# Packing 64 routed experts into 32 blocks of rows instead of 40, gathering four blocks at once, and spreading a normalisation over softmax groups

## The chip, the core and the metric

The kernel runs on one core of a Trainium2 chip. TensorE (PE) multiplies, VectorE (DVE), ScalarE (ACT) and GpSimd (POOL) do the rest, SyncE (SP) issues most DMAs; each runs its own instruction stream and they meet at semaphores. The metric is the device time of one execution in microseconds; the median of three before was 2076.38 us (2073.79 to 2079.16).

## The reference, cut to what matters

Two layers run over 384 tokens (128 context, 256 latent), width 1024, all in float32.

```
h = x * (1 + sc1) + sh1;  q,k,v,gate... = h @ w_in            # 1024 x 2816
ya = retention(4 heads x 64), both directions
     o = (o - mean) / sqrt(var + eps) per head; ya = (o * gn_g + gn_b) * silu(gate)
yb = windowed attention (6 heads),  yc = neighbourhood attention (6 heads)
x  = LN(alpha * x + g1 * (concat(ya, yb, yc) @ w_out))
h  = x * (1 + sc2) + sh2
scores = sigmoid(h @ w_router); 6 of 64 experts a token, group limited
routed = sum over the chosen e of  w_e * (silu(h @ gate_e) * (h @ up_e)) @ down_e
x  = LN(alpha * x + g2 * (routed + shared expert))
```

An expert has a 1024 x 512 matrix for gate and up (2 MB) and a 256 x 1024 matrix for down (1 MB). There are 384 x 6 = 2304 assignments a layer, 36 an expert on average.

## The kernel before, in words

A hardware loop runs the layer twice. A layer has these stages: modulation vectors, the combined input projection, retention, twelve softmax groups (each three heads of one 128-token tile; the first four groups are the context tile with 128 keys, the other eight have 384), the output projection, the first norm, routing, the routed experts with the shared one among them, and the second norm. Nothing is planned at run time: each engine's order is written out by hand, and waits are placed by semaphore.

**Retention's norm.** DVE evicts the state (L1209), and then runs the per-head norm of all three tiles in one go: mean (L1215), subtract, square, sum (L1219), variance (L1220), a square root on ACT (L1632), reciprocal and four multiplies and adds (L1222 to L1229). Only then does it start on the softmax groups, whose row maxima it takes with `peak` (L1238) and whose outputs it scales with `weigh` (L1257). ACT computes silu of the gate (L1630) and the root just ahead of its softmax work. PE has already computed the scores of groups 0 and 1 (L835) and waits with the transposes of group 0's weights (L856) for ACT's exponentials.

**Routing.** Experts 0 to 3 get a block of 128 rows each, at once (`PRE = 4`). The others are ordered by their count of tokens, highest first. DVE writes for each assignment a place; POOL scatters 36 / 2 = 18 columns of entries to a table in DRAM with one indirect DMA each (L1768), reads the table back (L1777), and DVE turns it into row indices (`take_slots`, L1439, L1440). An expert that gets more rows than its room sends the rest to further table columns, and if any has, a second loop over 3 x 64 blocks runs.

**The experts.** `BLOCKS` lists 40 blocks of 128 rows. After the four first ones, a pattern of 1, 2, 2 experts a block repeats: an expert alone has 128 rows of room, one of a pair has 64. For block b PE runs, in this order: `gate_up(b)` (L975: eight steps of k, one matmul for each expert of the block, its rows as weights, the expert's matrix as 512 moving columns, output to the partitions of its rows), `turn_rows(b+1)` (L961: transposes of the gathered rows), `down_rows(b-1)` (L1000), `turn_hidden(b)` (L985), and in twelve of the blocks a step of the shared expert (L1013 to L1025). ACT applies silu (L1703) and evicts the transposed rows (L1695, L1696), DVE multiplies (L1466), evicts the hidden rows (L1475) and the outputs (L1482, L1483). POOL gathers the rows of block b+2 (L1752) after the transposes of block b, and scatters the outputs of block b-1 (L1758). The four first gathers stand in POOL's stream as 0, 1, then eight of the 18 table scatters, 2, eight more, 3, and the last two.

**Weights.** SP loads gate and up into a ring of four 2 MB buffers (`NG`, L610) and down into six 1 MB buffers (`ND`, L614), in one stream: for block b it waits for `gate_up(b)`, issues the ring loads that go into the buffers which this frees, then waits for `down_rows(b-1)` and issues the down loads that this frees. Load n of the ring thus waits for `gate_up` of the block that holds load n-4. At block 36 SP also loads 2 MB of vectors for the second norm (L598, L600), at block 6 the shared expert's 3 MB. A matmul in float32 is two instructions in the trace.

## Time and profile before

| | |
|---|---|
| median of three runs | 2076.38 us |
| the profiled execution, time | 2074.37 us |
| the profiled execution, span | 2072.3 us |
| mean granted TensorE clock | 0.892 |
| PE busy | 82% of the span |
| HBM read, written | 573.53 MB, 48.81 MB |

The span runs from the first to the last instruction; the profiled execution's own time is 2.1 us more. The two layers take about half of the span each; in the page's 40 slices (51.8 us each) the experts of the first layer lie in slices 8 to 18 and those of the second in 28 to 38. Busy time of PE counts pipelined matmuls and is no measure of how near the array is to its peak.

### The profile page before, as it was taken

The numbers are of one execution on the slowest core, as the hardware profiler recorded it, in microseconds if no ns is written. First come the engines' busy times: TensorE is split into PE (matmuls) and PEld (weight loads), VectorE is DVE, ScalarE is ACT, GpSimd is POOL, SyncE is SP. The second block draws the span as 40 slices with busy tenths as digits, with TensorE's granted clock in tenths as the row PEclk, the third lists the DMA queues.
The fourth block names the chain that finished last, engine by engine and source line by source line (L and its number), as shares of the span: only waits on it lengthen the run. The fifth ranks groups of instructions, "written<-read, shape, count | busy, mean of one in ns | idle before, by whom it ended". The sixth has DMA issues, their size and how long they took to land. (4 is left out here: it accounts for less than half of the span.)

```text
span 2072.3 us, 19838 instructions
## 1 busy us (share of the span) xinstructions
PE 1692.1 (82%) x7193; PEld 875.9 (42%) x7193; DVE 593.9 (29%) x1190; ACT 340.2 (16%) x668; POOL 227.5 (11%) x228
## 2 busy tenths in 40 slices
PE   3897888779798999997348969887897989999953
PEld 1685563534333343342117746545433333433421
DVE  1525324621111111111615353255211111111116
ACT  0322341101110111010012224411110100101100
POOL 0000000141111111110000000002311111111100
PEclk8898699689899999999659987987898999999986
DMA  7634318179999999995475343171799999999944
GB/s 294 188 119 145 135 37 307 57 262 369 422 410 416 402 393 424 405 402 208 183 272 158 127 175 124 51 320 67 255 401 422 413 396 410 401 422 386 415 168 175
DMA packets 119282, 576.95 MB, mean 278 GB/s; under 512 B 46252, under 2 KB 48828, under 8 KB 78088
## 3 DMA queue, kind: packets, MB, share of 16 engines
q1 hardware_dynamic: 93992, 534.38, 64.9%
q0 software_dynamic: 25120, 41.13, 5.4%
q8 instruction: 62, 1.02, 0.2%
q14 instruction: 44, 0.36, 0.1%
q10 hardware_dynamic: 64, 0.07, 0.0%
HBM read 573.53 MB, written 48.81 MB: 300 GB/s over the span
## 5 line engine op out<-in xcount | busy, mean ns | idle before, releaser
L975 PE MATMUL bank<-ring,arena_a 128*64 128x512 f32 (+1 forms) x2048 | 592.3, 621 | 92.6 <-DMA ring<-in_w_expert_gu 89.0
L975 PEld LDWEIGHTS bank<-ring,arena_a 128*64 128x64 f32 (+1 forms) x2048 | 216.7, 156 | 424.1 <-issue 424.1
L1000 PE MATMUL bank<-arena_b,arena_a 128*64 128x512 f32 (+1 forms) x704 | 237.3, 604 | 2.7 <-DVE arena_a L1475 2.7
L1466 DVE SCALAR_TENSOR_TENSOR arena_a<-arena_a,slot_w,bank 128x256 f32<-128x256 f32 x80 | 38.5, 481 | 589.7 <-ACT arena_a L1703 583.0
L1758 POOL DMA_INDIRECT scratch_y<-arena_a,slot_idx x80 | 80.4, 1005 | 889.8 <-DVE arena_a L1483 889.2
L1703 ACT ACTIVATE arena_a<-bank 128x256 f32<-128x256 f32 x80 | 30.7, 384 | 889.8 <-PE bank L975 889.8
L1482 DVE COPY arena_a<-bank 128x512 f32<-128x512 f32 x80 | 55.3, 692 | 316.6 <-PE bank L1000 316.6
L760 PE MATMUL bank<-win_hi,xmT_hi 128*128 128x512 f32 (+1 forms) x288 | 110.0, 382 | 27.3 <-DVE arena_a L1122 24.6
L1000 PEld LDWEIGHTS bank<-arena_b,arena_a 128*64 128x64 f32 (+1 forms) x704 | 78.7, 154 | 101.4 <-issue 98.2
L1000 PE MATMUL bank<-arena_a 128*64 128x512 f32 (+1 forms) x320 | 116.4, 597 | 0.0
L761 PE MATMUL bank<-win_hi,xmT_lo 128*128 128x512 f32 (+1 forms) x288 | 110.5, 384 | 0.0
L961 PE MATMUL bank<-cst,arena_a 128*128 128x128 f32 x640 | 89.5, 285 | 25.4 <-DMA arena_a<-scratch_x,slot_idx 25.4
L762 PE MATMUL bank<-w_lo,xmT_hi 128*128 128x512 f32 (+1 forms) x288 | 110.0, 382 | 0.0
L961 PEld LDWEIGHTS bank<-cst,arena_a 128*128 128x128 f32 x640 | 73.6, 145 | 81.1 <-issue 54.3
L1752 POOL DMA_INDIRECT arena_a<-scratch_x,slot_idx x80 | 83.9, 1048 | 103.6 <-DVE slot_w L1383 54.8
L897 PE MATMUL bank<-ring,xmT 128*128 128x512 f32 x192 | 86.3, 613 | 7.5 <-ACTq L1670 7.5
L706 PE MATMUL bank<-ring,condT 128*2 128x512 f32 x384 | 61.3, 751 | 29.8 <-DMA ring<-in_w_mod 29.8
L1113 DVE TENSOR_TENSOR w_lo<-ring,win_hi 128x2048 fp32r<-128x2048 f32 (+1 forms) x24 | 55.6, 2318 | 80.0 <-ACT win_hi L1584 80.0
L760 PEld LDWEIGHTS bank<-win_hi,xmT_hi 128*128 128x128 f32 x288 | 55.3, 192 | 40.1 <-issue 24.8
L1695 ACT ACTIVATE arena_a<-bank 128x512 f32<-128x512 f32 x80 | 47.8, 597 | 122.1 <-PE bank L961 122.1
L1077 PE MATMUL bank<-ring,cst 128*128 128x512 f32 x72 | 36.4, 662 | 35.8 <-DMA ring<-scratch_y 31.7
L1584 ACT ACTIVATE win_hi<-ring 128x2048 fp32r<-128x2048 f32 (+1 forms) x24 | 42.3, 1771 | 134.9 <-PE bank L762 70.6
(263 smaller groups left out, 1710.2 us busy)
## 6 DMA issues: line engine op xcount, KB each, us to landing
ring<-in_w_expert_gu SPq DMA_DIRECT2D x128, 2048.0 KB, 18.7
arena_b<-in_w_expert_down SPq DMA_DIRECT2D x88, 1024.0 KB, 21.3
ring<-in_w_mod SPq DMA_DIRECT2D x24, 2048.0 KB, 7.7
arena_a<-in_w_expert_down SPq DMA_DIRECT2D x40, 1024.0 KB, 19.8
ring<-in_w_in SPq DMA_DIRECT2D x10, 2048.0 KB, 13.2
ring<-in_w_out SPq DMA_DIRECT2D x4, 2048.0 KB, 8.3
ring<-scratch_y SPq DMA_DIRECT2D x4, 2048.0 KB, 10.8
ring<-scratch_y SPq DMA_DIRECT2D x8, 1024.0 KB, 17.1
```

Source lines behind the costliest of these rows:

```text
L706: ins = pe.matmul(bank[32 * j:32 * j + 2, :], condT[:, k, :], w[:, k % 2, CH * j:CH * j + CH], start=(k == 0), stop=False)
L760: pe.matmul(out, hi[:, k, :], win_hi[:, k, cols], start=(k == 0), stop=False)
L761: pe.matmul(out, lo[:, k, :], win_hi[:, k, cols], start=False, stop=False)
L762: ins = pe.matmul(out, hi[:, k, :], w_lo[s][:, k, cols], start=False, stop=(k == KD - 1))
L897: ins = pe.matmul(bank[:, :], xmT[:, k, P * t:P * t + P], w[:, k, :], start=(k == 0), stop=(k == KD - 1))
L961: ins = pe.transpose(psum[2 + k // 4][:, P * (k % 4):P * (k % 4) + P], xg[b % 2][:, P * k:P * k + P], ident)
L975: ins = pe.matmul(psum[b % 2][w * i:w * i + w, :], xT[:, k, w * i:w * i + w], ring_view(gu_slot(n))[:, k, :], start=(k == 0), stop=(k == K ...
L1000: ins = pe.matmul(psum[5 + f][w * i:w * i + w, :], hT[b % 2][:, k, w * i:w * i + w], down[n % ND][:, k, CH * f:CH * f + CH], start=(k == 0 ...
L1113: dve.tensor_tensor(w_lo[s][:, ks, cols], ring_view(s)[:, ks, cols], win_hi[:, ks, cols].bitcast(F32), ALU.subtract).then_inc(win_lo_ready, 1)
L1482: dve.tensor_copy(ys[b % 2][:, 0:CH], psum[5][:, :])
L1752: pool.indirect_dma_start(xg[b % 2], None, scratch_x, bass.IndirectOffsetOnAxis(ap=slot_idx[:, 0, b:b + 1], axis=0), bounds_check=TOK - 1, ...
L1758: pool.indirect_dma_start(scratch_y, bass.IndirectOffsetOnAxis(ap=slot_idx[:, 1, b:b + 1], axis=0), ys[b % 2], None, bounds_check=TOK * TO ...
```

## The change

The first part is the plan of blocks: 32 blocks, of kind 1 (one expert, 128 rows), kind 2 (two of 64) and kind 3 (one of 64 and two of 32), after the four first ones. Ranks 4 to 11 get 128 rows, 12 to 39 get 64, 40 to 63 get 32. In a kind 3 block all matmuls are 32 rows wide, four for each step of k; the expert with 64 rows takes two of them. The rings stay as they are.

```diff
-    for _ in range(6):
-        for size in (1, 2, 2, 1, 2, 2):
...
+    blocks = [[(n, P)] for n in range(PRE)]
+    wide, half, third = iter(range(PRE, 12)), iter(range(12, 40)), iter(range(40, E))
+    for _ in range(4):
+        for kind in (3, 1, 3, 2, 3, 1, 2):
+            if kind == 1:
+                blocks.append([(next(wide), P)])
+            elif kind == 2:
+                blocks.append([(next(half), 64), (next(half), 64)])
             else:
-                blocks.append([paired, paired + 1])
-                paired += 2
+                blocks.append([(next(half), 64), (next(third), 32), (next(third), 32)])
...
-SHARED_AT = {13 + 2 * n: (n // 4, n % 4) for n in range(4 * TILES)}
-SHARED_LOAD, NORM_LOAD = 6, 36
+SHARED_AT = {8 + 2 * n: (n // 4, n % 4) for n in range(4 * TILES)}
+SHARED_LOAD, NORM_LOAD = 5, 29
...
+            def block_tiles(b):
+                loads, sizes = block_loads(b), [rows for r, rows in BLOCKS[b]]
+                w = min(sizes)
+                of_tile = [n for n, rows in zip(loads, sizes) for _ in range(rows // w)]
+                return [(n, w * i, w) for i, n in enumerate(of_tile)]
...
                     for k in range(KD):
-                        for i, n in enumerate(loads):
-                            ins = pe.matmul(psum[b % 2][w * i:w * i + w, :], xT[:, k, w * i:w * i + w], ring_view(gu_slot(n))[:, k, :],
+                        for n, r, w in block_tiles(b):
+                            ins = pe.matmul(psum[b % 2][r:r + w, :], xT[:, k, r:r + w], ring_view(gu_slot(n))[:, k, :],
                                             start=(k == 0), stop=(k == KD - 1))
```

`down_rows` changes in the same way. The second part: the four first gathers are issued at once, ahead of the table's scatters, into four buffers (the two of before and two that held the first norm's gates).

```diff
+            def gather_of(b):
+                if b < PRE:
+                    return (xg + [gateb[:, 0, :], gateb[:, 1, :]])[b], first_gathered[b], 16
+                return xg[b % 2], gathered[b % 2], 16 * ((b - PRE) // 2 + 1)
...
-                gather(0)
-                gather(1)
+                for b in range(PRE):
+                    gather(b)
...
-                    if j in (7, 15):
-                        b = 2 + j // 8
-                        pool.wait_ge(xT_full, b - 1)
-                        gather(b)
```

The third: for the last block `down_rows` of the block before comes ahead of `gate_up` on PE, and `rows_out` ahead of `hidden` on DVE.

```diff
+                    if b == NB - 1:
+                        down_rows(b - 1)
                     gate_up(b)
                     if b + 1 < NB:
                         turn_rows(b + 1)
-                    if b:
+                    if 0 < b < NB - 1:
```

The fourth: retention's norm becomes nine steps, one behind each softmax group's `weigh`; ACT takes silu of the gate ahead of retention, and the root behind the exponentials of group 5.

```diff
                     if g:
                         weigh(g - 1)
+                        retention_norm(g - 1)
...
+                    if g == 5:
+                        act.wait_ge(var_ready, 1)
+                        act.activation(var, var, ACT.Sqrt).then_inc(root_ready, 1)
```

Steps 0 to 3 are mean, subtract, square, variance; 4 is empty; 5 is reciprocal and multiply; 6 and 7 the learned scale and shift; 8 the multiply by the gate.

## Rows read from the trace of the kernel before

**Rows 1.** The page: DMA issues; count, KB each, median us to landing.
```profile
ring<-in_w_mod SPq DMA_DIRECT2D x24, 2048.0 KB, 7.7
```
**Rows 2.** Windows; columns PE, PEld, DVE, ACT, POOL busy, PE clock, DMA share, GB/s.
```profile
413.70:500.00 86.30, 73.16 (x247) 33.01 (x248) 18.86 (x31) 9.68 (x20) 29.70 (x29) 0.92 0.78 289
500.00:940.00 440.00, 405.32 (x1620) 166.01 (x1618) 71.40 (x136) 46.70 (x96) 62.65 (x62) 0.97 0.99 410
```
**Rows 3.** Waits of PE, 403 to 985: us in total, times, longest.
```profile
PE bank L975 <- DMA ring<-in_w_expert_gu: 43.8, 11, 11.0
```
**Rows 4.** Timeline of PE: a block of one expert, and the next, a pair.
```profile
464.90 7.03 PE L975 MATMUL bank<-ring,arena_a 128*128 128x512 f32 x16
...
476.39 7.09 PE L975 MATMUL bank<-ring,arena_a 128*64 128x512 f32 x32
```
**Rows 5.** Timeline of PE around the gathers of blocks 2 and 3.
```profile
414.66 7.11 PE L975 MATMUL bank<-ring,arena_a 128*128 128x512 f32 x16 [0.60 <-issue]
432.06 1.97 PE L961 MATMUL bank<-cst,arena_a 128*128 128x128 f32 x8 [10.29 <-DMA arena_a<-scratch_x,slot_idx]
433.82 5.76 PE L1000 MATMUL bank<-arena_b,arena_a 128*128 128x512 f32 x8
```
**Rows 6.** Timeline of POOL: first scatter of the table, and its reading back.
```profile
410.58 1.02 POOL L1768 DMA_INDIRECT slots<-arena_a,place_i  x1 [10.52 <-DVE place_i L1429]
...
438.72 0.60 POOL L1777 DMA_DIRECT2D arena_a<-slots  x1 [1.42 <-DMA slots<-arena_a,place_i]
```
**Rows 7.** Groups by line and form: weight loads of 64 and of 2 columns.
```profile
L975 PEld LDWEIGHTS bank<-ring,arena_a 128*64 128x64 f32 x1536 | 119.9, 144 | 305.7 <-issue 305.7
L706 PEld LDWEIGHTS bank<-ring,condT 128*2 128x2 f32 x384 | 7.4, 88 | 56.7 <-DMA ring<-in_w_mod 39.4 <-issue 15.4
```
**Rows 8.** Timeline of PE: 16 matmuls over four groups of 32 columns.
```profile
198.05 1.90 PE L706 MATMUL bank<-ring,condT 128*2 128x512 f32 x16
```
**Rows 9.** Timeline of PE: gate_up after waits for weights, and the layer's end.
```profile
534.57 10.05 PE L975 MATMUL bank<-ring,arena_a 128*64 128x512 f32 x32 [11.03 <-DMA ring<-in_w_expert_gu]
...
963.59 8.88 PE L975 MATMUL bank<-ring,arena_a 128*64 128x512 f32 x32 [7.20 <-DMA ring<-in_w_expert_gu]
...
977.61 3.65 PE L1000 MATMUL bank<-arena_b,arena_a 128*64 128x512 f32 x16 [1.34 <-DVE arena_a L1475]
```
**Rows 10.** Timeline of SP at the end of the experts.
```profile
929.95 0.91 SPq L598 DMA_DIRECT2D arena_b<-mods  x2
...
936.95 1.32 SPq L610 DMA_DIRECT2D ring<-in_w_expert_gu  x1
```
**Rows 11.** Timeline of all engines between retention and softmax.
```profile
202.03 0.68 DVE L1209 TENSOR_SCALAR arena_b<-bank 64x512 f32<-64x512 f32 x1 [3.51 <-PE bank L815]
...
211.69 0.68 DVE L1238 TENSOR_REDUCE cmisc<-bank 128x1 f32<-128x128 f32 x3
214.18 0.90 PE L856 MATMUL bank<-cst,arena_b 128*128 128x128 f32 x3 [11.31 <-ACTq L1661]
```
**Rows 12.** Windows of the softmax stage, columns as in rows 2.
```profile
226.00:247.00 21.00, 20.92 (x85) 13.75 (x85) 5.38 (x17) 4.29 (x16) 0.00 (x0) 0.50 0.29 101
```
**Rows 13.** Timeline of DVE: peak, and a group's weigh at either clock.
```profile
226.38 0.36 DVE L1257 TENSOR_TENSOR arena_a<-bank,cmisc 128x192 f32<-128x192 f32 x1 [3.74 <-PE bank L870]
236.97 0.36 DVE L1257 TENSOR_TENSOR arena_a<-bank,cmisc 128x192 f32<-128x192 f32 x1 [3.07 <-PE bank L870]
...
257.77 0.36 DVE L1257 TENSOR_TENSOR arena_a<-bank,cmisc 128x192 f32<-128x192 f32 x1 [3.40 <-PE bank L870]
259.37 0.56 DVE L1238 TENSOR_REDUCE cmisc<-bank 128x1 f32<-128x384 f32 x1 [1.24 <-PE bank L847]
...
266.33 0.36 DVE L1257 TENSOR_TENSOR arena_a<-bank,cmisc 128x192 f32<-128x192 f32 x1 [3.60 <-PE bank L870]
```
**Rows 14.** Timeline of ACT, second layer: waits for DVE's decay, silu's table.
```profile
1208.91 0.62 ACT L1620 ACTIVATE arena_b<-cst,cmisc 128x384 f32<-128x384 f32 x1 [5.05 <-DVE arena_b L1193]
...
1220.81 1.28 ACT L1630 ACT_TABLE_LOAD   x1
```

More of the change, by code:

```diff
@@ L40, in plan_blocks @@
 def plan_blocks():
-    blocks = [[n] for n in range(PRE)]
-    alone, paired = PRE, PRE + 12
-    for _ in range(6):
-        for size in (1, 2, 2, 1, 2, 2):
-            if size == 1:
-                blocks.append([alone])
-                alone += 1
-            else:
-                blocks.append([paired, paired + 1])
-                paired += 2
-    assert alone == PRE + 12 and paired == E
+    blocks = [[(n, P)] for n in range(PRE)]
[6 more added lines that the diff above has]
+                blocks.append([(next(half), 64), (next(half), 64)])
+            else:
+                blocks.append([(next(half), 64), (next(third), 32), (next(third), 32)])
+    assert all(next(left, None) is None for left in (wide, half, third))
     return blocks
@@ L59 @@
 NB = len(BLOCKS)
-LOADS = [r for b in BLOCKS for r in b]
+LOADS = [r for b in BLOCKS for r, rows in b]
 BLOCK_OF = [n for n, b in enumerate(BLOCKS) for r in b]
@@ L138, in constants @@
     for n, b in enumerate(BLOCKS):
-        for i, r in enumerate(b):
-            cap[r], row[r], col[r] = P // len(b), P // len(b) * i, n
+        for i, (r, rows) in enumerate(b):
+            cap[r], row[r], col[r] = rows, sum(other for _, other in b[:i]), n
     put("cap", cap[:, None])
@@ L426, in build @@
             gathered, scattered = [sem("gathered0"), sem("gathered1")], [sem("scattered0"), sem("scattered1")]
+            first_gathered = [sem(f"first_gathered{b}") for b in range(PRE)]
             xT_full, xT_ready, gu_full, silu_done, hid_ready = (
@@ L955, in turn_rows @@
                 def turn_rows(b):
-                    pe.wait_ge(gathered[b % 2], 16 * (b // 2 + 1))
+                    rows_in, landed, count = gather_of(b)
+                    pe.wait_ge(landed, count)
                     if b:
@@ L966, in gate_up @@
                     loads = block_loads(b)
-                    w = P // len(loads)
                     pe.wait_ge(xT_ready, b + 1)
@@ L990, in down_rows @@
                     loads = block_loads(b)
-                    w = P // len(loads)
                     pe.wait_ge(hT_ready, b + 1)
@@ L998, in down_rows @@
                         for k in range(2):
-                            for i, n in enumerate(loads):
-                                ins = pe.matmul(psum[5 + f][w * i:w * i + w, :], hT[b % 2][:, k, w * i:w * i + w],
+                            for n, r, w in block_tiles(b):
+                                ins = pe.matmul(psum[5 + f][r:r + w, :], hT[b % 2][:, k, r:r + w],
                                                 down[n % ND][:, k, CH * f:CH * f + CH], start=(k == 0), stop=(k == 1))
@@ L1485, in _ @@
                 for b in range(NB):
+                    if b == NB - 1:
+                        rows_out(b - 1)
                     hidden(b)
-                    if b:
+                    if 0 < b < NB - 1:
                         rows_out(b - 1)
@@ L1603, in _ @@
                         high_win(n + 1, 1)
+                act.wait_ge(h_dve, h_on_dve)
+                act.activation(h[:, :, GA:GA + 256], h[:, :, GA:GA + 256], ACT.Silu).then_inc(gate_ready, 1)
                 act.wait_ge(lg_ready, 1)
@@ L1628, in _ @@
                             act.sem_inc(kctxT_ready, 1)
-                act.wait_ge(h_dve, h_on_dve)
-                act.activation(h[:, :, GA:GA + 256], h[:, :, GA:GA + 256], ACT.Silu).then_inc(gate_ready, 1)
-                act.wait_ge(var_ready, 1)
-                act.activation(var, var, ACT.Sqrt).then_inc(root_ready, 1)
                 late_rows(0)
@@ L1789, in _ @@
                     pool.wait_ge(scattered[i], 16 * (NB // 2))
-                    pool.wait_ge(gathered[i], 16 * (NB // 2))
+                    pool.wait_ge(gathered[i], 16 * ((NB - PRE) // 2))
                 pool.wait_ge(most_ready, 1)
```

46 lines of the change are left out of this document (28 added, 18 removed).

## The prediction

> **What bounds the kernel.** I read the DMA issues of the page first, then windows, waits and timelines. A load of 2 MB into the ring lands 7.7 us after its issue in the modulation, where little else moves [rows 1]. The windows show what the experts' loads do: from 500 to 940 us the DMA share is 0.99 at 410 GB/s, while PE is busy 405 of 440 us; but from 413.7, when SP issues the first ring load after the four first ones, to 500 the share is only 0.78 [rows 2]. So in most of the stage DMA is the bound, and in its first 86 us DMA idles about 0.22 x 86.3 = 19 us. The waits of PE confirm it: 43.8 us in eleven waits for the experts' gate and up matrices [rows 3]. PE is not far behind: a block lasts 476.39 - 464.90 = 11.5 us, whether its gate_up takes 7.03 us with one expert or 7.09 with two [rows 4], so 40 blocks are 460 to 470 us and with the shared expert some 500, in a stage of about 580. By bytes at 410 GB/s, 2.10 MB for gate and up take 5.1 us and 1.05 MB for down 2.6, together 7.7 us an expert. A 3-block thus has 23.0 us of DMA against some 11.7 us of PE. Eight blocks fewer save 8 x 11.5 = 92 us of PE a layer, and I cost nearly all of this at nothing: DMA covers it. What counts is where DMA idles, what stands ahead of the last weights, and what follows them.
>
> **The four gathers.** Between gate_up of block 1 and the transposes of block 2 PE idles 10.29 us for the gather of block 2, which stands behind eight scatters of the table on POOL; then the clock is at its lower level, so the transposes take 1.97 us for 1.04 to 1.09 elsewhere and down_rows 5.76 for some 3.6 [rows 5]. With the gathers in front all this goes: 10.3 + 0.9 + 2.2 = 13.4 us in the first layer (some 11 in the second, by the same reading). What is late next is the gather of block 4, which needs the table. Twenty indirect DMAs from 410.58 to the read back at 438.72 take 1.34 us each with the last wait off [rows 6]; two fewer bring the table 2.7 us forward, and block 4's transposes would then wait 1 or 2 us, about as now. So PE reaches block 4 some 12 us earlier, and ring loads 6 and on go out 12 us earlier, into a stretch where DMA idles 19 us. I take -12 us a layer. Bounds: 0, if the idle stays somewhere else before 500, and -19, all of it.
>
> **The 32-wide tiles.** Four column groups at work at once appear in the modulation: 16 matmuls of 512 columns over four groups take 1.90 us [rows 8], which is three steps of 0.43 and a last one of 0.59. Weight loads take 88 ns for 2 columns and 144 for 64 [rows 7]; between them, 32 columns give some 115, and four in a row 460 ns against a step of 430. So gate_up of a 3-block should take 7.1 to 7.4 us, as the others do; the lower bound is the 7.03 of one expert, the upper, if the groups didn't overlap, twice that for pairs of groups, 14.2. I take 7.4. Up to some 9 us it lies under the 23.0 us of DMA but for what follows.
>
> The pair's gate_up shows weights of one column group being loaded while the other group's matmuls over the same rows of the array run: 32 instructions in 7.09 us against 16 in 7.03 [rows 4]. The Trainium skill ("TensorE: Matmul & The Clock Gate", section "The mechanism") states that a weight load overlaps running matmuls only where their row groups differ. By that rule a pair's step would be 2 x 144 + 430 = 0.72 us and its gate_up over 11, which this trace does not show; by it a 3-block would have a gate_up of 16 x (0.46 + 0.43) = 14.2 us, as in the first rival.
>
> **The ring under a 3-block.** This is where the change loses. A 3-block's gate_up holds three of four ring buffers, and SP issues nothing more until it has ended, since it stands at the wait for it. When its last matrix lands, what is still queued is one ring load (5.1 us) and one down load (2.6), with some 1.5 us of gathered and scattered rows: 9 us. gate_up then takes 7.4 us, or 9 to 10 after a wait, since the clock has fallen (10.05 us after a wait of 11.03, 8.88 after 7.20) [rows 9], and of the 7.7 us from issue to landing of a load that has the queue to itself 5.1 are its bytes, which leaves some 2.5 us in which nothing moves [rows 1]. So DMA runs dry 1 to 3.5 us. That holds only where little else is queued: a 3-block behind a pair, with one expert behind it (blocks 11, 18 and 25), and the first (block 4). The other eight 3-blocks follow one expert: the loads for it and for themselves were issued together, and four to six loads are queued. Four times 2.5 us: +10 a layer. Bounds: 0, and +30 where every 3-block runs dry by 2.5.
>
> **The end of the experts.** SP issues the 2 MB of the second norm's vectors at 929.95, ahead of the last ring load at 936.95, which lands at 963.6 [rows 9, 10]. In the new order that load comes behind the last ring load: -5.1 us. After it PE now needs 977.61 + 3.65 - 963.59 = 17.7 us, in which two down_rows stand; one of them moves under the wait for the weights: -3.6 us. The rows_out that moves with it goes the same way. The last down loads are queued behind the last ring loads as before. Together -9 (0 if block 30's down is itself late).
>
> **Sum for the experts:** -12 + 10 - 9 = -11 us a layer.
>
> **Retention's norm.** DVE's eviction of the state ends at 202.71 and its first peak starts at 211.69; PE idles 11.31 us until 214.18 [rows 11]. With the norm moved the peak can start at once: -8.9. The steps go behind `weigh`, each about 1 us. In the eight large groups DVE idles 1.24 us before the next peak even at full clock [rows 13], and PE at low clock is busy 20.92 of 21 us [rows 12]; they are hidden, and if they weren't each cost 1 us. In the small context groups the next peak follows at once, so steps 0 and 1 cost 0.8 us each: +1.5. The clock: in 226 to 247 it is at 0.50 after that idle stretch, and a large group takes 236.97 - 226.38 = 10.6 us, at full clock 266.33 - 257.77 = 8.6 [rows 12, 13]. With an idle stretch of some 2.5 us in place of 11.3 it may not fall; two groups and the small ones would give 5. I count 2: -2. The root with its table is put where ACT waits for PE. Silu ahead of retention adds a table load of 1.28 us where ACT later waits 5.05 us for DVE's decay [rows 14]: 0, and 3 if the first decay were on the path. Sum: -8.9 + 1.5 - 2 = -9.4 a layer; bounds -14 and -4.
>
> **The whole:** 2 x (-11 - 9.4) = -41 us. The profiled execution took 2074.4 us (its span and 2.1 us around it), so 2033; the median of the runs is 2.0 above it, so I say 2035.
>
> **Rivals.** *The column groups don't overlap (slower).* In each of 12 3-blocks gate_up takes 14.2 and down_rows 7.2. Then DMA has 9 us queued under a gate_up of 14.2 + 2: dry by some 7 us twelve times, +84, where 10 is counted; against that the waits for DMA shorten, so I take half of it, +45. The layer then changes by -20.4 + 45 - 10 = +15 to twice that: about 2120 us. It decides from a gate_up of about 11 us. Against it speak rows 8. Chance 4%. *Every 3-block runs the ring dry.* The remaining eight lose 2.5 to 3 us too: +20 to +24 a layer, which gives 2076 to 2083. For it: SP's stream blocks at the wait for the long gate_up. Against: the queue behind one expert is longer. Chance 8%, half of it above 2082. *The start is given back.* DMA stays the bound and the earlier loads only lengthen the waits of PE, experts -2 a layer: 2 x -11.4, 2053 us. Chance 16%. *Nothing runs dry, and the clock stays up in softmax.* -12 - 9 and -13 a layer: 2008 us. Chance 15%. *An expert exceeds its room*, and the 192 further blocks run, at no less than 7.7 us of weights each, 1.5 ms a layer. Reckoned from the reference's inputs, the largest counts are 107 for ranks 4 to 11, 55 for ranks 12 to 39 and 28 for ranks 40 to 63, so rooms of 128, 64 and 32 hold. Under 1%.
>
> **How the numbers follow.** The forecast has 57% (2018 to 2048). The range for 8 in 10 takes in the third rival and most of the fourth: 2003 to 2066. A change of 0.3%, 6 us, is what can be told from none. Faster is the forecast, the third and fourth rivals, 88%; slower the first, half of the second, and a little for what I don't see, 7%; same 5%.
>
> **What would show it.** PE: no wait before the transposes of block 2, and one before block 4's; the peak behind the state's eviction, an idle stretch of 2.5 us there; gate_up with four tiles in 7.1 to 7.4 us (9 to 10 after waits). PE's waits for the ring about 120 us a layer instead of 44, and yet an earlier end. DMA share above 0.9 in the first 86 us, with short dips behind 3-blocks 4, 11, 18 and 25. It would be wrong if dips stood behind all twelve, if gate_up took over 9 us with no wait before it, or if the stage began earlier and ended at the same time.

## The result, and the profile after

The changed kernel takes 2058.76 us in the median of 7 runs (2052.78 to 2065.12), the kernel before 2079.16 (2073.79 to 2084.35) beside it: ratio 0.9903, 95% interval 0.9879 to 0.9927, so 20 us faster. The forecast was 41 to 44 us. The profiled execution took 2062.63 us with a span of 2060.9. Ratios below are all to the kernel before in the same session; 0.001 is 2.1 us.

I split both profiled executions at four points of each layer: DVE's eviction of the state, gate_up of block 0, gate_up of block 4, the end of the last down_rows.

| stretch, us (layer 1 / layer 2) | before | after | change | forecast |
|---|---|---|---|---|
| eviction of the state to gate_up(0) | 201.5 / 197.3 | 197.2 / 194.9 | -4.3 / -2.4 | -9.4 |
| gate_up(0) to gate_up(4) | 61.4 / 60.7 | 54.3 / 57.2 | -7.1 / -3.5 | -12 |
| gate_up(4) to the end of the experts | 516.4 / 517.2 | 518.2 / 518.6 | +1.8 / +1.4 | +10 - 9 |
| all else (three stretches) | 517.9 together | 520.6 | +2.7 | 0 |

The sum is -11.4, the difference of the two spans. The medians differ by 20.4: the profiled execution before lay 4.8 us below its median, and this one lies 3.9 above.

The page first. PE waits for ring loads 248.7 us in the two layers, and a ring load takes 15.7 us from issue to landing in the median, where one with the queue to itself took 7.7 [rows 1] (in the kernel before the ring loads took 18.7, so waiting in the queue is not new):
```profile
L992 PE MATMUL bank<-ring,arena_a 128*32 128x512 f32 (+2 forms) x2432 | 509.3, 675 | 252.4 <-DMA ring<-in_w_expert_gu 248.7
...
ring<-in_w_expert_gu SPq DMA_DIRECT2D x128, 2048.0 KB, 15.7
```
PE's waits from 403 to 985 us, to be read against [rows 3]: 125.6 us for 43.8, as forecast (about 120).
```profile
PE bank L992 <- DMA ring<-in_w_expert_gu: 125.6, 15, 21.6
PE bank L979 <- DMA arena_a<-scratch_x,slot_idx: 4.9, 1, 4.9
```
Windows (PE, PEld, DVE, ACT, POOL busy, PE's clock, DMA share, GB/s), against [rows 2]: the share rose from 0.78 to 0.89 in the first stretch and fell from 0.99 to 0.94 in the second, where three windows of 20 us have dips:
```profile
413.70:500.00 86.30, 69.31 (x318) 31.14 (x316) 17.60 (x30) 8.71 (x18) 24.70 (x26) 0.94 0.89 351
500.00:940.00 440.00, 325.54 (x1734) 124.24 (x1736) 52.37 (x100) 34.97 (x72) 44.46 (x44) 0.86 0.94 391
580.00:600.00 20.00, 10.61 (x72) 3.53 (x72) 0.41 (x1) 0.39 (x1) 0.00 (x0) 0.63 0.68 285
720.00:740.00 20.00, 16.63 (x98) 6.13 (x99) 2.43 (x5) 1.47 (x3) 0.63 (x1) 0.80 0.58 227
860.00:880.00 20.00, 20.00 (x114) 7.96 (x110) 2.58 (x5) 2.94 (x6) 2.02 (x2) 0.98 0.67 265
```
PE's timeline: gate_up of block 0; the transposes, down_rows and gate_up around block 4, against [rows 4, 5]; and the end, against [rows 9]. The long wait for a gather now stands ahead of block 4 (4.91 us, and 9.07 in the second layer, for 2.25 and 2.30 before), and the last gate_up waits for nothing:
```profile
399.32 9.23 PE L992 MATMUL bank<-ring,arena_a 128*128 128x512 f32 x16 [1.22 <-issue]
...
446.63 1.97 PE L979 MATMUL bank<-cst,arena_a 128*128 128x128 f32 x8 [4.91 <-DMA arena_a<-scratch_x,slot_idx]
448.39 5.10 PE L1016 MATMUL bank<-arena_b,arena_a 128*128 128x512 f32 x8
...
453.63 7.07 PE L992 MATMUL bank<-ring,arena_a 128*32 128x512 f32 x64
...
959.09 7.09 PE L992 MATMUL bank<-ring,arena_a 128*64 128x512 f32 x32
...
968.13 3.65 PE L1016 MATMUL bank<-arena_b,arena_a 128*64 128x512 f32 x16 [0.52 <-DVE arena_a L1505]
```
POOL's timeline, against [rows 6]: the last scatter of the table, its reading back, and the gather of block 4, which lands when PE's transposes start, 446.63 - 440.94 = 5.7 us on.
```profile
428.32 0.98 POOL L1802 DMA_INDIRECT slots<-arena_a,place_i  x1 [0.30 <-issue]
433.71 0.60 POOL L1807 DMA_DIRECT2D arena_a<-slots  x1 [4.42 <-DMA slots<-arena_a,place_i]
...
440.94 1.04 POOL L1786 DMA_INDIRECT arena_a<-scratch_x,slot_idx  x1 [5.33 <-DVE slot_w L1470]
```
Before the change the same gather landed 4.3 us after its issue, 2.2 us ahead of SP's ring load (timelines of PE, POOL and SP):
```profile
460.32 1.09 PE L961 MATMUL bank<-cst,arena_a 128*128 128x128 f32 x8 [2.25 <-DMA arena_a<-scratch_x,slot_idx]
...
456.04 1.04 POOL L1752 DMA_INDIRECT arena_a<-scratch_x,slot_idx  x1 [12.80 <-DVE slot_w L1440]
...
458.29 0.33 SPq L610 DMA_DIRECT2D ring<-in_w_expert_gu  x1
```
Groups by form, against [rows 7]: a weight load of 32 columns takes 125 ns; the estimate was 115.
```profile
L992 PEld LDWEIGHTS bank<-ring,arena_a 128*32 128x32 f32 x1536 | 60.3, 125 | 266.9 <-issue 266.9
```
DVE's timeline, against [rows 11, 13]: the peak follows the eviction at once, 8.6 us earlier, but two `weigh` (L1286) stand 12.8 us apart where 8.6 is a group at full clock:
```profile
202.13 0.68 DVE L1227 TENSOR_SCALAR arena_b<-bank 64x512 f32<-64x512 f32 x1 [3.51 <-PE bank L832]
203.05 0.69 DVE L1267 TENSOR_REDUCE cmisc<-bank 128x1 f32<-128x128 f32 x3 [0.24 <-DVE arena_b L1227]
...
247.74 0.36 DVE L1286 TENSOR_TENSOR arena_a<-bank,cmisc 128x192 f32<-128x192 f32 x1 [3.40 <-PE bank L887]
...
260.50 0.36 DVE L1286 TENSOR_TENSOR arena_a<-bank,cmisc 128x192 f32<-128x192 f32 x1 [4.40 <-PE bank L887]
```

### The profile page after: what moved, and what is told of

It reads as the page before. It is cut to its first block and busy times, and to the rows that moved or that the text cites. A ratio compares the mean times of both kernels' runs of the same rounds, so it can differ in the third digit from the quotient of the medians.

```text
span 2060.9 us, 20342 instructions
## 1 busy us (share of the span) xinstructions
PE 1543.4 (75%) x7609; PEld 797.3 (39%) x7609; DVE 563.4 (27%) x1126; ACT 316.7 (15%) x620; POOL 194.0 (9%) x196
## 5 line engine op out<-in xcount | busy, mean ns | idle before, releaser
L992 PE MATMUL bank<-ring,arena_a 128*32 128x512 f32 (+2 forms) x2432 | 509.3, 675 | 252.4 <-DMA ring<-in_w_expert_gu 248.7
L992 PEld LDWEIGHTS bank<-ring,arena_a 128*32 128x32 f32 (+2 forms) x2432 | 175.0, 142 | 553.8 <-issue 553.5
L1016 PE MATMUL bank<-arena_b,arena_a 128*32 128x512 f32 (+2 forms) x800 | 206.1, 600 | 1.9 <-DVE arena_a L1505 1.9
L1792 POOL DMA_INDIRECT scratch_y<-arena_a,slot_idx x64 | 63.5, 992 | 935.0 <-DVE arena_a L1513 933.7
L1016 PE MATMUL bank<-arena_a 128*32 128x512 f32 (+2 forms) x416 | 116.0, 595 | 0.0
L1016 PEld LDWEIGHTS bank<-arena_b,arena_a 128*32 128x32 f32 (+2 forms) x800 | 62.0, 131 | 66.6 <-issue 62.9
L979 PE MATMUL bank<-cst,arena_a 128*128 128x128 f32 x480 | 68.0, 287 | 15.9 <-DMA arena_a<-scratch_x,slot_idx 15.9
L979 PEld LDWEIGHTS bank<-cst,arena_a 128*128 128x128 f32 x480 | 55.7, 146 | 58.8 <-issue 43.2
L1786 POOL DMA_INDIRECT arena_a<-scratch_x,slot_idx x60 | 63.3, 1055 | 81.0 <-DVE slot_w L1413 54.7
L778 PEld LDWEIGHTS bank<-win_hi,xmT_lo 128*128 128x128 f32 x288 | 55.9, 194 | 11.1
## 6 DMA issues: line engine op xcount, KB each, us to landing
ring<-in_w_expert_gu SPq DMA_DIRECT2D x128, 2048.0 KB, 15.7
ring<-scratch_y SPq DMA_DIRECT2D x4, 2048.0 KB, 10.7
```

The source lines that it names most:

```text
L778: pe.matmul(out, lo[:, k, :], win_hi[:, k, cols], start=False, stop=False)
L979: ins = pe.transpose(psum[2 + k // 4][:, P * (k % 4):P * (k % 4) + P], rows_in[:, P * k:P * k + P], ident)
L992: ins = pe.matmul(psum[b % 2][r:r + w, :], xT[:, k, r:r + w], ring_view(gu_slot(n))[:, k, :], start=(k == 0), stop=(k == KD - 1))
L1016: ins = pe.matmul(psum[5 + f][r:r + w, :], hT[b % 2][:, k, r:r + w], down[n % ND][:, k, CH * f:CH * f + CH], start=(k == 0), stop=(k == 1))
L1786: pool.indirect_dma_start(rows_in, None, scratch_x, bass.IndirectOffsetOnAxis(ap=slot_idx[:, 0, b:b + 1], axis=0), bounds_check=TOK - 1, o ...
L1792: pool.indirect_dma_start(scratch_y, bass.IndirectOffsetOnAxis(ap=slot_idx[:, 1, b:b + 1], axis=0), ys[b % 2], None, bounds_check=TOK * TO ...
```

## The experiments

Each changes only what its diff shows (long ones shortened). Ratios with their 95% intervals:

| kernel | ratio | experts, us, layers 1 / 2 |
|---|---|---|
| before | 1 | 577.8 / 577.9 |
| changed | 0.9903 (0.9879 to 0.9927) | 572.5 / 575.8 |
| forty blocks | 0.9786 (0.9753 to 0.9820) | 556.9 / 557.9 |
| order mixed | 0.9748 (0.9707 to 0.9788) | 554.1 / 560.8 |
| order bunched | 1.0144 (1.0099 to 1.0189) | 598.6 / 605.4 |
| root last | 0.9843 (0.9806 to 0.9880) | 569.3 / 572.9 |
| norm alone | 0.9950 (0.9931 to 0.9970) | 577.7 / 580.7 |
| norm undone | 0.9934 (0.9894 to 0.9974) | 573.6 / 569.5 |
| gathers alone | 0.9977 (0.9945 to 1.0008) | 574.0 / 573.7 |
| gathers undone | 0.9927 (0.9903 to 0.9951) | 578.8 / 582.8 |
| end alone | 0.9897 (0.9849 to 0.9944) | 567.4 / 570.3 |

One sum orders these rows. In all 18 profiles the busy time of the DMA engines (the share times the length), from gate_up(0) to the end of the experts, is 517 to 524 us a layer, whatever the plan of blocks. What differs is their idle time: 55.5 and 56.1 us before, 53.2 and 56.9 in the changed kernel, 37.0 twice with forty blocks, 35.1 and 41.5 with the mixed order, 79.7 and 87.3 with the bunched one. A change of the experts is worth what it takes from this idle time.

### The blocks: forty again

```diff
-        for kind in (3, 1, 3, 2, 3, 1, 2):
+        for kind in (1, 2, 2, 1, 2, 2):        # six times; ranks 4 to 15 alone, 16 to 63 in pairs
```
`SHARED_AT` and `SHARED_LOAD` stand as before the change; `NORM_LOAD` is 37, behind the last ring load.

> The changed kernel with the forty blocks of before (1, 2, 2, 1, 2, 2), and all the rest of the change (gathers, end of the experts, retention's norm). Theory (the new blocks cost by the ring under the blocks of three, more than their 92 us less of PE bring): the experts are 12 us a layer shorter than with the new blocks, 2035 us, and PE's waits for the ring are 30 to 50 us a layer. Rival (PE's 92 us are what gives the kernel its gain): slower than the changed kernel, 2065 us or more.

Measured: 0.9786 (2033.27 us in the median), 0.0117 or 24 us below the changed kernel, 12 a layer, and 32.9 us of waits for the ring in the first layer. The theory holds, and the rival (2065 us or more) falls. From gate_up(4) to the end it lasts 506.4 and 507.2 us for 518.2 and 518.6. So the new blocks cost 11.8 and 11.4 us a layer; the forecast put 10 on them. The largest part of the change makes it slower, and eight blocks less of PE's work bring nothing in this order.

### The order of the blocks

```diff
-        for kind in (3, 1, 3, 2, 3, 1, 2):
+        for kind in (2, 1, 3, 2, 3, 1, 3):      # mixed
+        for kind in (3, 3, 1, 2, 3, 2, 1):      # bunched
```

> The changed kernel with one edit: the seven kinds of block that repeat four times stand in the order 2, 1, 3, 2, 3, 1, 3 instead of 3, 1, 3, 2, 3, 1, 2. Blocks, rooms, bytes and instructions are the same. Theory (the ring runs dry for 6.5 to 8.4 us under blocks 11, 18 and 25, and about as long again behind block 4, because so little is queued when the last matrix of a block of three lands): in this order a block of three never follows a pair that follows a single one, the three dips of the DMA share (0.68, 0.58, 0.67 in a window of 20 us) go, and the experts last 15 to 20 us less a layer: 2019 to 2029 us. Rival A (the dips come from the length of a block of three itself, wherever it stands): the dips stay in number and size, 2055 to 2062 us. Rival B (DMA contention sets the whole stage and the dips are made up later): dips go, time 2050 us or more.

> The changed kernel with the order of kinds 3, 3, 1, 2, 3, 2, 1. Theory of the dry ring: two blocks of three stand side by side, and each time the second waits for all its weights with nothing behind them: more and longer dips, 20 to 26 us more a layer, about 2100 to 2110 us. Rival A (order does not matter): 2059 us.

Measured: 2022.94 and 2108.21 us in the medians (the second of two runs only, both above every run of any other kernel), both within the theory's bounds. The same blocks in another order differ by 0.0396, 82 us (85 by the medians). The window that had 0.94 in the changed kernel (500 to 940) shows 0.98 with the mixed order (to 920, as its stage is shorter):
```profile
500.00:920.00 420.00, 331.57 (x1772) 129.24 (x1776) 54.49 (x104) 35.45 (x74) 45.53 (x45) 0.89 0.98 408
```
and 0.92 with the bunched one:
```profile
500.00:940.00 440.00, 297.16 (x1588) 114.45 (x1586) 51.43 (x98) 32.18 (x67) 44.52 (x44) 0.84 0.92 382
```
Rivals A and B fall. The mechanism can be read behind block 11 of the changed kernel. SP issues two ring loads and one down load, and then nothing until gate_up(11) has ended:
```profile
569.66 1.50 SPq L627 DMA_DIRECT2D ring<-in_w_expert_gu  x2
574.11 0.33 SPq L631 DMA_DIRECT2D arena_a<-in_w_expert_down  x1
599.95 2.68 SPq L627 DMA_DIRECT2D ring<-in_w_expert_gu  x3
```
On PE, gate_up(11) starts when its last matrix lands:
```profile
589.39 9.71 PE L992 MATMUL bank<-ring,arena_a 128*32 128x512 f32 x64 [15.05 <-DMA ring<-in_w_expert_gu]
```
and in windows of 2 us (the last two columns again DMA share and GB/s) the engines run out under it:
```profile
590.00:592.00 2.00, 2.00 (x16) 0.53 (x12) 0.00 (x0) 0.00 (x0) 0.00 (x0) 0.50 0.90 379
592.00:594.00 2.00, 2.00 (x16) 0.60 (x12) 0.00 (x0) 0.00 (x0) 0.00 (x0) 0.50 0.60 246
594.00:596.00 2.00, 2.00 (x20) 0.59 (x16) 0.00 (x0) 0.00 (x0) 0.00 (x0) 0.81 0.30 127
596.00:598.00 2.00, 2.00 (x24) 0.59 (x20) 0.00 (x0) 0.00 (x0) 0.00 (x0) 1.00 0.02 8
598.00:600.00 2.00, 2.00 (x20) 0.99 (x12) 0.41 (x1) 0.39 (x1) 0.00 (x0) 1.00 0.00 0
600.00:602.00 2.00, 2.00 (x12) 0.77 (x12) 0.07 (x1) 1.08 (x2) 0.00 (x0) 1.00 0.70 147
```
After the landing there are 2 x (0.90 + 0.60 + 0.30) = 3.6 us of DMA work and some 0.6 before 590, 4.2 in all; I had reckoned 9 queued. The two ring loads were issued together and ran side by side. By the trace's DMA records, what was still to start at 589.39 was 0.7 MB in the 16 KB packets of the ring loads, a third of the second one, and 1.0 MB in the 8 KB packets of the down load, nearly all of it; I had counted the second ring load whole. Under blocks 18 and 25 less was left, 2.8 and 3.2 us of work. What is missing is 10.6 - 4.2 = 6.4 us. The three dips come to 6.4, 8.4 and 6.6 us by the shares of their windows (0.68, 0.58, 0.67 of 20 us), not to 2.5 each.

### The root of the variance

```diff
-                    if g == 5:
+                    if g == len(soft) - 1:
                         act.wait_ge(var_ready, 1)
                         act.activation(var, var, ACT.Sqrt).then_inc(root_ready, 1)
...
+                    if g == len(soft):
+                        for step in range(5, 9):
+                            retention_norm(step)
                     if g:
                         weigh(g - 1)
-                        retention_norm(g - 1)
+                        if g < 5:
+                            retention_norm(g - 1)
```

> The changed kernel with the root of retention's variance moved on ACT from behind the exponentials of softmax group 5 to behind those of the last group, and the steps 5 to 8 of the norm on DVE ahead of the last group's weigh. Theory (the root's two table loads, 2 x 1.28 us, delay the exponentials of group 6, PE then idles and its clock falls to the lower level for the next 8 us): the exponentials of group 6 start 1.3 us earlier, the clock stays at 1.00 from 240 to 290 us in the first layer, and the kernel is 4 to 5 us a layer faster: 2049 to 2051 us. Rival A (the clock falls there for another reason): -1.3 us a layer or less, 2056 to 2059 us. Rival B (four steps in one place hold the last weigh back): 2059 to 2065 us.

Measured: 0.9843, 0.0060 or 12.5 us below the changed kernel, about 6 a layer (the intervals overlap by a hair). That is more than the 4 to 5 us of the theory, and not all of it is the root's: the experts are 3.2 and 2.9 us shorter too, where the gather of block 4 landed 4.4 and 5.0 us after its issue for 5.7 and 7.4. In the changed kernel ACT loads the root's table and 6.5 us later that of the exponential again:
```profile
240.04 1.28 ACT L1696 ACT_TABLE_LOAD   x1
...
246.56 1.28 ACT L1682 ACT_TABLE_LOAD   x1
```
The second load has no cover: the exponentials of group 6 wait for it, PE idles 1.1 of the 5 us from 245 (3.90 busy), and then its clock is at the lower of its two levels for 5 us and more:
```profile
245.00:250.00 5.00, 3.90 (x28) 2.91 (x26) 1.54 (x3) 4.30 (x10) 0.00 (x0) 1.00 0.92 314
250.00:255.00 5.00, 5.00 (x14) 2.33 (x14) 1.11 (x2) 0.00 (x0) 0.00 (x0) 0.50 0.30 110
```
With the root behind the last group the same stretch shows:
```profile
245.00:250.00 5.00, 5.00 (x32) 2.48 (x31) 1.92 (x5) 0.29 (x1) 0.00 (x0) 1.00 0.64 240
250.00:255.00 5.00, 4.94 (x40) 4.10 (x37) 0.92 (x2) 2.98 (x9) 0.00 (x0) 1.00 0.49 67
```
Of all the kernels run, those with the root behind group 5 show this fall, 44 to 52 us after the eviction, in 13 of 14 layers, those with the root last in none of 14. From the eviction to gate_up(0) the means are 199.9 us with the norm in one piece (8 layers), 193.2 with the root behind group 5 (14) and 189.2 with the root last (14). In six of the seven kernels with the root last, steps 0 to 3 stand elsewhere too, but the one where they don't has 187.8 and 190.8. Nor is it the luck of the clock at the start of the stage: of the layers where the clock was back 34 to 36 us after the eviction, those with the root behind group 5 took 194.8 to 199.6 us (5) and those with the root last 190.5 to 192.2 (9). The whole run has 21 table loads with the root behind group 5, as before the change, and 17 with it last.

### The norm alone, and undone

The fourth part of the change put into the kernel before; and taken out of the changed kernel, so that norm, root and silu stand as before.

> The kernel before with the fourth part of the change alone: retention's norm in steps behind the softmax groups, the root behind group 5, silu ahead of retention. Theory: the stretch from the state's eviction to the first gate_up, 201.5 and 197.3 us before, falls to the 191 to 197 us that kernels with this part have shown, so -6 to -10 us a layer and 2057 to 2065 us. Rival (retention's part earns only what the profile of the changed kernel has, 4.3 and 2.4 us a layer): 2070 us.

> The changed kernel with its fourth part undone: retention's norm in one piece ahead of the softmax groups. Theory (from the state's eviction to the first gate_up the part gives 7.6 us a layer in the mean of the profiles, less what experts take back): 10 to 15 us slower than the changed kernel, ratio 0.995 to 0.998. Rival (the 18.8 us of the forecast): ratio 0.999.

Measured: alone 0.9950 (2067.83 us, between theory and rival), so 10 us; undone 0.9934 for 0.9903, so 6 us, less than the 10 to 15 of the theory, but with 10 us of uncertainty. By the profiles it is 199.9 - 193.2 = 6.7 us a layer, 13 in all, of which the whole kernel keeps 6 to 10. The forecast was 19.

### The gathers alone, and undone

> The kernel before with the second part alone: the four first gathers at once, ahead of the table's scatters. Theory: -12 us a layer, as forecast, the experts last 566 us instead of 578: 2053 us. Rival (the gain shows only where the end of the stage is shortened too, since DMA bounds what lies between): -3 us a layer or less, 2070 us or more.

> The changed kernel with its second part undone: two gathers ahead of the table's scatters, those of blocks 2 and 3 among them, as before. In the changed kernel gate_up of block 4 starts 54.3 us after that of block 0 in the first layer and 57.2 in the second, for 61.4 and 60.7 before. Theory (the part is worth this difference, 7.1 and 3.5 us, since the gather of block 4 then waits for the table): 10 us slower than the changed kernel, ratio 0.995 to the kernel before. Rival A (the 12 us a layer of the forecast are there and other parts lost them): ratio 1.002 or more. Rival B (worth nothing, as nearly in the run of this part alone, 0.9977): 0.990 to 0.992.

Measured: alone 0.9977, 5 us, which can't be told from nothing, so that the theory (2053 us) falls; undone 0.9927, 5 us slower than the changed kernel, with 7 of uncertainty, so that it doesn't tell theory and rival B apart; rival A falls. The stages tell more: the experts are 3.8 and 4.2 us shorter alone, 6.3 and 7.0 us longer undone, 8 to 13 us for both layers. Alone, PE's timeline has the wait of [rows 5] again, two blocks later:
```profile
456.60 1.97 PE L968 MATMUL bank<-cst,arena_a 128*128 128x128 f32 x8 [9.13 <-DMA arena_a<-scratch_x,slot_idx]
```
and the windows show hardly more DMA work in the first stretch than before (0.79 for 0.78):
```profile
413.70:500.00 86.30, 75.37 (x261) 34.63 (x260) 20.99 (x34) 10.18 (x21) 27.32 (x29) 0.94 0.79 297
```

### What the gather of block 4 waits for

First, SP's ring load behind gate_up(2) held until the table is back:
```diff
+                    if b == 2:
+                        sp.wait_ge(table_loaded, 16)
```

> The changed kernel with one wait more: SP issues the ring load that follows gate_up of block 2 only when the table has been read back (about 5 us later). Theory (the read back and the gather of block 4 are late because the experts' loads, which now run in the same stretch, fill the same DMA engines): POOL waits 1.4 us for the last scatter instead of 4.4, the gather lands 4.2 us after its issue instead of 5.7 to 7.4, PE waits some 3 us ahead of block 4 in both layers instead of 4.9 and 9.1, and the time moves by less than 0.3%, since the loads start that much later. Rival (the chain from the scatters to the gather does not depend on the loads): waits of PE as in the changed kernel.

Measured: 0.9868 (0.9815 to 0.9920), not to be told from the changed kernel. The gather was issued 39.8 and 38.9 us after gate_up(0), 2 to 4 us earlier, but landed 10.3 and 10.4 us later: PE waited 8.2 and 8.1 us. The theory was wrong where it held the load; the gather went into a fuller queue. Over all profiles a rule stood out, and I tried to use it, with a wait of SP ahead of the ring load that follows gate_up(3):
```diff
+                    if b == 3:
+                        sp.wait_ge(gather_issued, 1)
...
                         gather(b + 2)
+                        if b + 2 == PRE:
+                            pool.sem_inc(gather_issued, 1)      # "ahead"
                     if b:
                         scatter(b - 1)
+                    if b + 2 == PRE:
+                        pool.sem_inc(gather_issued, 1)          # "clear": here, not above
```
The kernels that it goes into have the root last and steps 0 to 3 of the norm behind `weigh` of the large groups 4 to 7. Without it:

> The kernel with the forty blocks, and the rest of the change, with the root behind the last group and steps 0 to 3 of the norm behind weigh of groups 4 to 7. Theory (0.9786 with the root behind group 5, and -0.0060 as it gave in the changed kernel): 0.970 to 0.974. Rival (the experts give it back): 0.976 or more.

> The changed kernel with two repairs: the order of kinds 2, 1, 3, 2, 3, 1, 3, and the root behind the last group's exponentials; steps 0 to 3 of the norm stand behind weigh of groups 4 to 7, which are large, and no longer of 0 to 3. Theory (the two gains, 0.9748 and 0.9843 against 0.9903, add up, and the steps leave the small groups, -1.5 us a layer): 0.967 to 0.970 of the time before, 2007 to 2013 us. Rival (what retention gives is taken back by the experts, which DMA bounds): 2019 us or more.

Measured: 0.9749 (0.9698 to 0.9800) and 0.9728 (0.9686 to 0.9770), 2029.02 and 2021.10 us: 0.0037 and 0.0020 below the kernels without it, for the 0.0060 that the root gave in the changed kernel; the theory of the sum fails in the second, where the time is the rival's, and in the first the ratio lies between the two. The forty blocks show why: their experts went from 556.9 and 557.9 us to 565.0 and 565.1, and gate_up(4) from 50.5 and 50.7 us after gate_up(0) to 57.3 and 57.9. With the wait, right behind the gather's issue:

> The kernel with forty blocks and the root behind the last group, where PE waited 9.03 and 8.94 us for the gather of block 4, with one wait more: SP issues the ring load that follows gate_up of block 3 only when POOL has issued that gather. In the profiles so far the gather lands 4.2 to 5.7 us after its issue where it went ahead of this 2 MB load (issued at 41.4 us from gate_up of block 0) and 7.3 to 10.4 us where it went behind it or behind a backlog. Theory (the gather queues behind the ring load on the same DMA engines, and this is what is left of the 12 us of the forecast): it lands within 5 us in both layers, PE waits 3 to 4 us ahead of block 4, and the experts last 557 to 560 us instead of 565: 8 to 14 us faster than 0.9749 of before, so 0.968 to 0.971. Rival (the gather is late for the chain of the table alone): PE waits 8 to 9 us as before the edit, ratio 0.973 to 0.977.

> The same wait on SP in the kernel with the order of kinds 2, 1, 3, 2, 3, 1, 3 and the root behind the last group, where PE waited 9.0 and 2.6 us ahead of block 4. Theory: 3 to 4 us in both layers, 3 to 6 us faster: ratio 0.969 to 0.971. Rival (DMA bounds the rest of the stage and takes it back): no change, 0.973.

Measured: 0.9722 (0.9684 to 0.9760) and 0.9717 (0.9675 to 0.9759); the gather landed late, 8.8 to 9.2 us after its issue, in three of four layers. The wait did not do what I wanted: SP's load still went out 0.1 to 1.1 us behind the gather's issue. Both ratios fall short of the theories. With the release behind the next scatter:

> The wait of SP once more, with its release behind the scatter that follows the gather of block 4 on POOL, not right behind the gather, so that the ring load goes out some 2 us behind the gather's issue. In 26 layers of the profiles so far the gather landed in 4.2 to 5.7 us wherever its issue stood 0.9 us or more ahead of this load's (11 layers), and in 7.3 us or more where it stood less far ahead or behind (13), but for two layers with a held load just ahead of it; in the last run it stood 0.1 to 0.8 us ahead. Theory (the gather's descriptors take about its 1.04 us on POOL, and a load that goes out before they are there goes first): it lands within 5.5 us in both layers, PE waits 2.5 to 4.5 us ahead of block 4, and the experts last 557 to 561 us. Rival (backlog from the loads before sets it, the distance only goes with it): still 8 to 10 us in one layer or both.

> The same in the kernel with the mixed order and the root behind the last group, where the gather landed 9.2 and 8.8 us after its issue. Theory: within 5.5 us in both layers, PE 4 us earlier at block 4, ratio 0.969 to 0.971 if the experts keep it. Rival (DMA bounds the rest and takes it back, or the backlog sets the landing): ratio 0.972 or more.

(The count in the first text is wrong: it is 24 layers, 11 of them landing early, 11 late and the two with the held load.) Measured: landings of 4.4, 4.2, 4.5 and 4.5 us in four of four layers, waits of PE 2.2 to 2.5 us; 0.9723 (0.9674 to 0.9773) and 0.9707 (0.9661 to 0.9752). The theory on the landing holds and the rival on the backlog falls; the gain in time isn't shown: the forty blocks' experts took 558.1 and 563.3 us, the second longer than the 561 of the theory, and neither ratio can be told from the one without the wait, though 0.9707 lies where its theory has it. The late landings say the same from the other side. Counted from the gather's issue they vary from 7.3 to 9.5 us, but counted from the issue of the ring load they come after 8.4 to 8.9 us in 11 of 11 layers: the gather lands when that load is through. The three lines that decide, from the timelines of PE, POOL and SP. In forty blocks the gather's issue stands 1.5 us ahead of the load's and it lands 4.2 us on:
```profile
439.24 1.67 PE L977 MATMUL bank<-cst,arena_a 128*128 128x128 f32 x8 [2.86 <-DMA arena_a<-scratch_x,slot_idx]
...
435.08 1.05 POOL L1784 DMA_INDIRECT arena_a<-scratch_x,slot_idx  x1 [5.12 <-DVE slot_w L1468]
...
436.60 0.33 SPq L625 DMA_DIRECT2D ring<-in_w_expert_gu  x1
```
with the root last (forty and root) 0.7 us ahead, and 9.5 us on:
```profile
444.27 1.97 PE L977 MATMUL bank<-cst,arena_a 128*128 128x128 f32 x8 [9.03 <-DMA arena_a<-scratch_x,slot_idx]
...
434.76 1.04 POOL L1788 DMA_INDIRECT arena_a<-scratch_x,slot_idx  x1 [5.84 <-DVE slot_w L1472]
...
435.46 0.33 SPq L625 DMA_DIRECT2D ring<-in_w_expert_gu  x1
```
and with the load held clear of it, 2.2 us ahead and 4.4 us on:
```profile
439.52 1.09 PE L980 MATMUL bank<-cst,arena_a 128*128 128x128 f32 x8 [2.43 <-DMA arena_a<-scratch_x,slot_idx]
...
435.07 1.04 POOL L1791 DMA_INDIRECT arena_a<-scratch_x,slot_idx  x1 [6.83 <-DVE slot_w L1475]
...
437.31 0.33 SPq L626 DMA_DIRECT2D ring<-in_w_expert_gu  x1
```
The kernel with the mixed order, the root last and the load held clear is the fastest here, 2015.68 us in the median, 0.9707: it beats before and the changed kernel. Against the mixed order alone (0.9748) the intervals overlap, so what the root and the held load add there isn't shown by the times.

### The end of the experts alone

```diff
-SHARED_LOAD, NORM_LOAD = 6, 36
+SHARED_LOAD, NORM_LOAD = 6, 37
```
with the order of the last block as in the change.

> The kernel before with the third part alone: the second norm's vectors behind the last ring load, down_rows of the last block but one ahead of the last gate_up. Theory: -9 us a layer, as forecast, the experts last 569 us: 2059 us. Rival (the last down load comes last anyway): -3 us a layer, 2071 us.

Measured: 0.9897, so 21 us (the interval allows 12 to 31), and the experts 10.4 and 7.6 us shorter. The theory holds. This small part alone does as much as the whole change.

## Why the prediction was wrong

Faster was right, and the result is in the range, but the gain is half of what I forecast. By the steps:

**The four gathers: this step failed.** "Block 4's transposes would then wait 1 or 2 us", I wrote, "I take -12 us a layer". PE did reach block 4 early, but waited 2.2 to 9.5 us for the gather there in the kernels with the new gathers. I moved the table by the issue of its scatters alone and carried over the landing times of a stretch in which few loads run. Two things were missed. The chain behind the scatters (read back, landing, DVE's cast, the gather's landing) is longer than PE's way to block 4 even at its best: with an early landing PE waits 2.2 to 4.9 us. And in 11 of 24 layers the gather went behind the 2 MB ring load that follows gate_up(3), which comes at that time only because PE is earlier: before, the gather's issue stood 2.2 us ahead of it and landed 4.3 us on. In the mean of the profiles gate_up(4) starts 62.3 us after gate_up(0) with the old gathers (8 layers), 52.3 with the new ones and an early landing (11), and 57.4 with a late one (11): -10 or -5 for the -12. The profiled execution of the changed kernel had one of each. The experts keep 8 to 13 us of it where the step had 24. How much they keep depends on the rest: in forty blocks the 7 us of a late gather go through to the end; with the gathers alone the 6.8 us of the second layer shrank to 4.2, and why, the runs leave open.

**Retention's norm: the step on the root failed.** The start of the first peak is right: 8.6 us earlier for 8.9. "The root with its table is put where ACT waits for PE" holds for the first table load and not for the second, which reloads the exponential's table in front of group 6 (above). I took its cost at 0 and it is 4.0 us a layer by the means, a fall of the clock included. Then 199.9 - 189.2 = 10.7 us, without it, is near the 9.4 I had. The -2 for the clock came at most in part in the profiled execution: the clock was back at 236 us for 247 before, and 8.6 us of that is the earlier start. PE idled 2.58 us ahead of group 0's transposes, as forecast (2.5), and the clock was at the lower level from 206 us all the same. In 7 of the other 12 layers with the same code in this stage it was back 8 us or more sooner.

**The ring under a block of three: right in sum, by luck; wrong in its parts.** +11.8 and +11.4 us a layer by forty blocks for +10. Three of the four places are right (blocks 11, 18 and 25), and the size of each is 6.4 to 8.4 us and not 2.5, since 2.8 to 4.2 us of work were queued and not 9. Behind block 4 there is no dip of its own: DMA idles 3.7 us in the 20 us from gate_up(4), and 4.5 with forty blocks. So three dips make 21 us, and some 10 of them come back. The traces say where, though not why: from gate_up(4) to the end DMA idles 36.2 us for 22.1 with forty blocks (layer 1) and works 482.0 for 484.3, so there are 7 us less of idle time outside the dips, nearly half of it at the very end, and 2 us less work. The earlier start of the loads is not the reason, as forty blocks have it too (a share of 0.90 from 413.7 to 500 us, for 0.89).

**The end of the experts: right.** -9 forecast, -10.4 and -7.6 alone (-10.1 and -10.2 from gate_up(4) on). The last gate_up waits for nothing, where it waited 7.20 us before [rows 9], and 971.78 - 959.09 = 12.7 us follow it, where 17.7 did.

**The 32-wide tiles: right.** gate_up 7.07 us for 7.1 to 7.4, down_rows 3.6. The trace agrees with the row on pairs [rows 4] and not with the rule that the Trainium skill states in "TensorE: Matmul & The Clock Gate", section "The mechanism", that only a difference of row groups lets them overlap: the weight loads of the four column groups, 125 ns each over the same rows of the array, are hidden, or gate_up would take over 14 us. The same section of the Trainium skill also lets a load into the background weight buffer go ahead of running matmuls, and with that the trace doesn't conflict.

**The sum.** By the runs: blocks +24, end -21, norm -6 to -10, gathers -5 (-8 to -13 by the stages), together -8 to -20 with 5 to 10 us of uncertainty on each, and -20 measured for all at once. Forecast: +20, -18, -19, -24. The two terms that were right cancel each other; the whole gain had to come from the two of which half or less came true. That the sum still lies in the range is owed to its width.

**The rivals.** None of them is what happened. (Their chances don't quite add up either: 4% and half of 8% for slower is more than the 7% given.) "The start is given back" came out at nearly the right time (2053 us) with a mechanism that the trace shows only in part: the start wasn't given back later so much as not gained.

## What to carry to other kernels

When a transfer moves earlier, time it with the traffic that the earlier start brings, and not with the landing time that it had before. Where blocks of different size share a ring of buffers, work out for each order what is queued when the last matrix lands: here the order was worth 82 us between the two tried, and the sizes 24. An ACT function with a table of its own among exponentials costs two table loads, 1.28 us each here, and what waits for the second; put it where the table has to change anyway, as the root behind the last group does.

## What the runs showed of the hardware

A gather of 128 rows of 4 KB and a 2 MB ring load on the same DMA engines don't share them evenly: with its issue 1.0 us or more ahead of the load's, the gather landed after 4.2 to 5.7 us in 15 of 15 layers with the new gathers (and 4.3 to 4.5 in the 8 with the old ones, 2.2 us ahead); from 0.8 us ahead to 1.5 us behind, after 7.3 to 9.5 us in 11 of 11, which is 8.4 to 8.9 us after the load's issue (the two layers with the load of gate_up(2) held, 10.3 and 10.4 us, stand apart). POOL's instruction for the gather itself lasts 1.04 us, about this bound; that the descriptors are ready only then is my reading, the trace doesn't show it.

TensorE's granted clock was at its lower level in 590 to 594 us, with PE busy all the time, after 15.05 us of waiting, and back at 1.00 from 596. And one stage falls into a few patterns of it: the softmax stage with the root behind group 5, the same code in seven kernels, took 194.8 to 199.6 us where the clock was back 34 or 35 us after the eviction (5 layers), 191.0 to 192.5 where it was back after 24 to 26 us (6), and 188.7 after 15 us (1). A profile of one execution can mislead by 4 us a layer there; means over 8 to 14 layers told the effects apart.
